# A hybrid decoder layer in split float32: high and low x in one matmul, projections in passes of 256 columns, shorter routing

## The reference

```python
def hybrid_mixer(n, w_in, conv_a_w, ssd_conv_w, ssd_conv_b, ssd_dt_bias, ssd_a_log, ssd_d,
                 ssd_norm_w, w_branch_a, w_branch_b, w_branch_c, w_out):
    u = n @ w_in
    u_a, u_b, u_c, u_g = jnp.split(u, [A_IN, A_IN + B_IN, A_IN + B_IN + SSD_IN], axis=-1)
    y_a = short_conv_mixer(u_a, conv_a_w) @ w_branch_a
    y_b = stick_breaking_attention(u_b) @ w_branch_b
    y_c = mamba2_ssd(u_c, ssd_conv_w, ssd_conv_b, ssd_dt_bias, ssd_a_log, ssd_d, ssd_norm_w) @ w_branch_c
    g_a, g_b, g_c = jnp.split(jax.nn.sigmoid(u_g), 3, axis=-1)
    return (g_a * y_a + g_b * y_b + g_c * y_c) @ w_out
...
    s = jnp.einsum('thcd,hcnd->thcn', q, sub_keys, preferred_element_type=jnp.float32)
    s1, i1 = lax.top_k(s[:, :, 0], PEER_TOPK)
    s2, i2 = lax.top_k(s[:, :, 1], PEER_TOPK)
    cand_s = (s1[..., :, None] + s2[..., None, :]).reshape(ntok, PEER_HEADS, PEER_TOPK * PEER_TOPK)
    cand_i = (i1[..., :, None] * PEER_NKEYS + i2[..., None, :]).reshape(ntok, PEER_HEADS, PEER_TOPK * PEER_TOPK)
    top_s, pos = lax.top_k(cand_s, PEER_TOPK)
```

## Time and profile before

| what | value |
|---|---|
| median of three runs | 3543.44 us |
| the profiled execution's own time | 3542.42 us |
| its span | 3540.7 us |
| PE matmuls busy, weight loads busy | 97%, 89% |
| DVE, ACT, GpSimd busy | 64%, 49%, 1% |
| granted TensorE clock, mean | 0.997 |
| DMA | 178 GB/s |
| A projection | 19.2 to 311.3 us |
| GA, to | 493.8 |
| B with first GB units, to | 815.6 |
| GB, to | 993.4 |
| C, to | 1511.1 |
| GC, w_out and query, to | 1797, 1880, 1987 |
| expert-down, expert-up, to | 2829, 3541 |

### The profile page before, as it was taken

The page is one execution under the profiler, slowest core; times in us unless marked ns, Lnnn a source line. Parts: engine busy times, 40 slices in busy tenths (PEclk is TensorE's granted clock), DMA queues, the critical chain, the costliest instruction groups (busy, mean ns, idle before and its releaser), DMA issues.

```text
span 3540.7 us, 69279 instructions
## 1 busy us (share of the span) xinstructions
PE 3448.7 (97%) x23037; PEld 3166.9 (89%) x23037; DVE 2274.7 (64%) x2901; ACT 1722.0 (49%) x2494; POOL 26.6 (1%) x32
## 2 busy tenths in 40 slices
PE   7999999999999999999999999999999999999998
PEld 7999889998899999978879989899999988887887
DVE  4555444454557777774545999988889855554555
ACT  4444434444445445454445434447777644444444
POOL 0000000000000000000000000000000000000000
PEclk9999999999999999999999999999999999999999
DMA  6666665556666555556677567576666677667665
GB/s 176 176 176 176 189 177 156 157 159 179 192 193 181 175 178 175 172 155 193 189 195 208 149 161 177 157 183 159 159 160 159 164 196 192 193 192 219 195 194 166
DMA packets 484119, 628.62 MB, mean 178 GB/s; under 512 B 76832, under 2 KB 341504, under 8 KB 481792
## 3 DMA queue, kind: packets, MB, share of 16 engines
q1 hardware_dynamic: 483968, 626.59, 64.4%
HBM read 622.03 MB, written 4.26 MB: 177 GB/s over the span
## 4 chain that ended last, share of the span: by engine, by line
PE 79%; DVE 9%; DMA 3%; ACT 3%; issue 3%; SPq 2%; DVEq 0%; ACTq 0%
PE bank L79 25%; PE bank L81 25%; PE bank L80 25%; DVE f_lo L126 2%; PE bank L1715 2%; DVE w_lo L1561 2%; PE bank L2122 2%; DVE w_raw L1554 1%; DMA w_raw<-in_peer_down 1%; SPq L451 1%; DMA f_raw<-in_w_in 1%; DVE c_xc L1182 1%; ACT f_hi L121 1%; DMA f_raw<-in_w_out 0%; SPq L458 0%
## 5 line engine op out<-in xcount | busy, mean ns | idle before, releaser
L126 DVE TENSOR_TENSOR f_lo<-f_raw,f_hi 128x768 fp32r<-128x768 f32 (+2 forms) x640 | 749.2, 1175 | 716.0 <-ACT f_hi L121 715.3
L121 ACT ACTIVATE f_hi<-f_raw 128x768 fp32r<-128x768 f32 (+2 forms) x640 | 646.2, 1016 | 749.3 <-DMA f_raw<-in_w_in 505.4
L79 PE MATMUL bank<-xT_hi,f_hi 128*128 128x256 f32 x2560 | 739.0, 289 | 26.6 <-DVE f_lo L126 11.6
L80 PE MATMUL bank<-xT_lo,f_hi 128*128 128x256 f32 x2560 | 724.3, 283 | 0.0
L81 PE MATMUL bank<-xT_hi,f_lo 128*128 128x256 f32 x2560 | 724.3, 283 | 0.0
L79 PE MATMUL bank<-xT_hi,w_hi 128*128 128x256 f32 x2048 | 590.4, 288 | 19.8 <-DVE w_lo L1561 19.7
L80 PE MATMUL bank<-xT_lo,w_hi 128*128 128x256 f32 x2048 | 579.1, 283 | 0.0
L81 PE MATMUL bank<-xT_hi,w_lo 128*128 128x256 f32 x2048 | 579.0, 283 | 0.0
L1653 DVE TENSOR_TENSOR w_lo<-w_raw,w_hi 128x1024 fp32r<-128x1024 f32 x256 | 313.5, 1225 | 340.8 <-PE bank L81 331.9
L79 PEld LDWEIGHTS bank<-xT_hi,f_hi 128*128 128x128 f32 x2560 | 490.7, 192 | 41.2 <-DVE f_lo L126 16.6
L80 PEld LDWEIGHTS bank<-xT_lo,f_hi 128*128 128x128 f32 x2560 | 491.0, 192 | 1.8 <-issue 1.7
(11 more groups left out here) (268 smaller groups left out, 4856.3 us busy)
## 6 DMA issues: line engine op xcount, KB each, us to landing
w_raw<-in_peer_down SPq DMA_DIRECT2D x1024, 128.0 KB, 3.4
w_raw<-in_peer_up SPq DMA_DIRECT2D x1024, 128.0 KB, 2.6
f_raw<-in_w_in SPq DMA_DIRECT2D x1024, 96.0 KB, 2.4
f_raw<-in_w_in SPq DMA_DIRECT2D x256, 256.0 KB, 2.9
f_raw<-in_w_in SPq DMA_DIRECT2D x384, 128.0 KB, 2.8
f_raw<-in_w_branch_c SPq DMA_DIRECT2D x256, 128.0 KB, 2.8
f_raw<-in_w_branch_a SPq DMA_DIRECT2D x128, 128.0 KB, 2.8
f_raw<-in_w_branch_b SPq DMA_DIRECT2D x128, 128.0 KB, 2.8
```

What stands on the lines that cost most here:

```text
L79: nc.tensor.matmul(out, lhs[0], rhs[0], start=start, stop=False, skip_group_check=True)
L80: nc.tensor.matmul(out, lhs[0], rhs[1], start=False, stop=False, skip_group_check=True)
L121: nc.scalar.activation(self.hi[u % 4][:, 0:cols], self.raw[u % 4][:, 0:cols], ACT.Copy).then_inc(self.hi_done, 1)
L126: nc.vector.tensor_tensor(self.lo[u % 4][:, 0:cols], self.raw[u % 4][:, 0:cols], self.hi[u % 4][:, 0:cols].bitcast(F32), ALU.subtract).the ...
```

## The change

High and low x lie in one tensor `xT`, and `pair_matmul` does high weight by high and low x in one matmul of 512 columns, then low weight by high x over 256 columns into the bank's first half. A block's sum thus fills a whole bank: the first half holds two of the three products, the second the third. The projections run in passes of two blocks: a unit is 4 x 128 rows by 256 columns (1024 columns of a slot, which shrinks from 1280), a pass has four units. A has 3 passes an iteration (12 units), C 5 (20 units), B 2 and a third for v with `tri_matmul` (12). At the end of a pass ACT copies the second half out (`part_a`, `part_qk`, `part_c`) behind the split of the next pass's first unit, and DVE adds the first (`sum_a`, `sum_qk`, `sum_c`).

In C the SSD work is placed anew, all of an iteration's chain within the next: SiLU of x at unit 0, of z at 2, clamp at 3 and 5 (on ACT now, as Relu with a negative scale over one head each), exponents at 4 and 6, PE's turn at 2, states 5, outputs 8, square sum 12; the convolution's first tap goes to ACT (`taps` at 11, 12, 17) and the other three stay on DVE at 14 to 19. In B z moves from 3 to 0, ACT's softplus from 6 to 1, the rest along with it; in GB from unit 4 to 2.

In routing, the rows of keys start a unit earlier and, from unit 32, come every second unit. Of the 256 sums of a head only the 64 that can be in the best 16 are formed, in four rectangles (`RECTS`), two heads at a time. The picks take two instructions a unit from 58 to 97; their ranks are worked back with arithmetic (`side_step`, 98 to 110), and 32 look-ups and 8 reductions (`look_up`, `add_hits`) stand for the 24 keys steps. Three copies after the routing go from DVE to ACT.

```diff
...
-        xT_hi = sb(top, "xT_hi", [P, KD, T], F32R)
-        xT_lo = sb(top, "xT_lo", [P, KD, T], F32R)
+        xT = sb(top, "xT", [P, 2, KD, T], F32R)
+        xT_hi, xT_lo = xT[:, 0, :, :], xT[:, 1, :, :]
+
+        def pair_matmul(out, lhs, k, start, stop):
+            both = out[:, :].rearrange("p (s t) -> p s t", s=2)
+            nc.tensor.matmul(both, lhs[0], xT[:, :, k, :], start=start, stop=False, skip_group_check=True)
+            return nc.tensor.matmul(both[:, 0, :], lhs[1], xT_hi[:, k, :], start=False, stop=stop,
+                                    skip_group_check=True)
...
-                def evacuate_a(p):
-                    act.wait_ge(fl.used, U_AB * p + U_AB)
-                    nc.scalar.activation(c_sb[:, :], bank[1][:, :], ACT.Copy).then_inc(a_evac, 1)
-                    nc.scalar.activation(b_sb[:, :], bank[0][:, :], ACT.Copy).then_inc(a_evac, 1)
+                def part_a(p, r):
+                    act.wait_ge(fl.used, U_AB * p + 4 * r + 4)
+                    for j in range(2):
+                        dst = (c_sb[:, j * T:(j + 1) * T], gate_hid[:, j, 2:T + 2], b_sb[:, j * T:(j + 1) * T])[r]
+                        if r == 1 and first_p(p) and j == 0:
+                            act.wait_ge(a_pad, 1)
+                        nc.scalar.activation(dst, bank[A_PASS[r][1 + j]][:, T:2 * T], ACT.Copy).then_inc(a_part, 1)
...
+                def part_c(p, r):
+                    act.wait_ge(fl.used, C0 + UN * p + 4 * r + 4)
+                    if first_p(p) and r == 0:
                         act.wait_ge(ssd["pad"], 1)
-                    for i in range(3):
-                        nc.scalar.activation(xpad[:, 2 * i:2 * i + 2, 3:T + 3],
-                                             bank[2 + i][:, :].rearrange("p (j t) -> p j t", j=2),
-                                             ACT.Copy).then_inc(ssd["evac"], 1)
-                    for i in range(2):
-                        nc.scalar.activation(zs[:, 2 * i:2 * i + 2, :],
-                                             bank[i][:, :].rearrange("p (j t) -> p j t", j=2),
-                                             ACT.Copy).then_inc(ssd["evac"], 1)
+                    for j in (2 * r, 2 * r + 1):
+                        dst = xpad[:, j, 3:T + 3] if r < 3 else zs[:, j - 6, :]
+                        nc.scalar.activation(dst, bank[C_BANK[j]][:, T:2 * T], ACT.Copy).then_inc(ssd["part"], 1)
...
+                def clamp(p, ch):
+                    act.wait_ge(ssd["ecs"], p + 1)
+                    for h in range(HPG):
+                        here = wts[:, ch, h, :]
+                        nc.scalar.activation(here, here, ACT.Relu, bias=cs_col[:, ch, ds(HPG * p + h, 1)],
+                                             scale=-1.0).then_inc(ssd["clamp"], 1)
+
                 def exp_w(p, ch):
-                    for q in range(2):
-                        act.wait_ge(ssd["min"], 4 * p + 2 * ch + q + 1)
-                        here = wts[:, ch, 4 * q:4 * q + 4, :]
-                        nc.scalar.activation(here, here, ACT.Exp).then_inc(ssd["exp"], 1)
+                    act.wait_ge(ssd["clamp"], 2 * HPG * p + HPG * (ch + 1))
+                    nc.scalar.activation(wts[:, ch, :, :], wts[:, ch, :, :], ACT.Exp, scale=-1.0).then_inc(ssd["exp"], 1)
...
+                def sum_c(p, r):
+                    for j in (2 * r, 2 * r + 1):
+                        here = xpad[:, j, 3:T + 3] if r < 3 else zs[:, j - 6, :]
+                        dve.wait_ge(ssd["part"], 10 * p + j + 1)
+                        nc.vector.tensor_tensor(here, here, bank[C_BANK[j]][:, 0:T], ALU.add).then_inc(ssd["evac"], 1)
...
+                def pass_unit(i, banks):
+                    for kk in range(4):
+                        k = 4 * i + kk
+                        for b in range(2):
+                            at = slice(kk * 256 + b * P, kk * 256 + b * P + P)
+                            last = pair_matmul(banks[b], (fl.hi[i][:, at], fl.lo[i][:, at]), k,
+                                               start=k == 0, stop=k == KD - 1)
+                    last.then_inc(fl.used, 1)
+
                 def a_unit(it, u, begin):
+                    r = u // 4
                     fl.wait_unit(pe, U_AB * it + u)
-                    for m in (2, 3, 0, 1, 4, 5):
-                        if u == 0 and not begin:
-                            if m == 2:
-                                pe.wait_ge(a_evac, 2 * it - 1)
-                            if m == 0:
-                                pe.wait_ge(a_evac, 2 * it)
-                            if m == 4:
-                                pe.wait_ge(a_gh, it)
-                        at = slice(m * P, (m + 1) * P)
-                        last = tri_matmul(bank[m // 2][:, (m % 2) * T:(m % 2 + 1) * T],
-                                          (fl.hi[u % 4][:, at], fl.lo[u % 4][:, at]), (xT_hi[:, u, :], xT_lo[:, u, :]),
-                                          start=u == 0 and m % 2 == 0, stop=u == KD - 1)
-                    last.then_inc(fl.used, 1)
+                    if u % 4 == 0 and not begin:
+                        pe.wait_ge(a_sum, 6 * it - 6 + 2 * r + 2)
+                    pass_unit(u % 4, (bank[A_PASS[r][1]], bank[A_PASS[r][2]]))
...
                 with act.Fori(1, N_AB) as it:
                     for u in range(U_AB):
-                        fl.split_hi(act, B0 + U_AB * it + u, B0 // 4 + 4 * it, u, W_AB)
-                        if u == 0:
-                            copy_qk(it - 1)
-                        if u == 6:
+                        fl.split_hi(act, B0 + U_AB * it + u, B0 // 4 + 3 * it, u, 1024)
+                        if u == 1:
                             softplus(it - 1)
-                        if u == 12:
+                        if u in (4, 8):
+                            part_qk(it, u // 4 - 1)
+                        if u == 7:
                             weights_b(it - 1)
-                        if u == 15:
+                        if u == 10:
                             o_hi_b(it - 1)
                 branch_split("gb", GB0, KD, GB_PAIRS, gb_hook)
...
+                def pick_row(g):
+                    if 13 <= g < QU:
+                        return g - 13
+                    return 19 + (g - QU) // 2 if QU <= g < QU + 26 and (g - QU) % 2 == 0 else None
+
...
+                def sums(q):
+                    r = head(2 * q)
+                    for i0, i1, nj, at in RECTS:
+                        ni = i1 - i0
+                        v.tensor_tensor(cand[:, r:r + 2, at:at + ni * nj].rearrange("p h (a b) -> p h a b", b=nj),
+                                        sides[:, r:r + 2, 0, i0:i1].unsqueeze(3).to_broadcast([P, 2, ni, nj]),
+                                        sides[:, r:r + 2, 1, 0:nj].unsqueeze(2).to_broadcast([P, 2, ni, nj]),
+                                        ALU.add).then_inc(t_cand, 1)
+
+                def best_step(o):
...
+                def look_up(side, a):
+                    dve.wait_ge(t_side, (7, 13)[side])
+                    dve.wait_ge(t_diff, 2)
+                    k = 0 if a < 4 else 4 if a < 8 else 8
+                    ranks = side_f[:, side, :].rearrange("p (r k) -> p r k", k=PK)
+                    v.scalar_tensor_tensor(out=hit[side][:, a, :, k:PK], in0=ranks[:, :, k:PK], scalar=float(a),
+                                           in1=keys_of[:, :, side, a:a + 1].to_broadcast([P, R, PK - k]),
+                                           op0=ALU.is_equal, op1=ALU.mult).then_inc(t_hits[side], 1)
+
...
+                def add_hits(side, c):
+                    dve.wait_ge(t_hits[side], PK)
+                    k0, k1, a, r0, r1 = ((0, 4, 4, 0, R), (4, 8, 8, 0, R), (8, 16, 16, 0, PH), (8, 16, 16, PH, R))[c]
+                    v.tensor_reduce(key_of[:, side, :].rearrange("p (r k) -> p r k", k=PK)[:, r0:r1, k0:k1],
+                                    hit[side][:, 0:a, r0:r1, k0:k1].rearrange("p a r k -> p r k a"),
+                                    AX.X, ALU.add).then_inc(t_red, 1)
 
                 def q_lo(n):
...
```

747 lines of the change are left out of this document (388 added, 359 removed).

## The result

The changed kernel takes **3608.5 us**, the median of four runs (3606.2 to 3612.0), against 3541.8 for the kernel before in the same comparison: a ratio of **1.019** (95% interval 1.0174 to 1.0206), some 67 us slower. The forecast was 3554 and its range ended at 3581: the direction was right, the size was wrong, and the time lies outside the range. The profiled execution took 3611.95 us.

A forecast was written before the change was run, and what follows sets the result against it. It took TensorE (PE), 79% of the chain, to bound the kernel, and DVE the routing. Terms of -14.6, +4, +1.4, +41.8, +3.5, -25 and 0.5 in the query phase gave +11.6 on 3542.4: 3554 us, range 3514 to 3581.

The forecast's parts named there:

- Term 4, C: C stage: a period grows from 65.9 to 71.6 us through PE's waits for splits; +41.8 us, the merged matmul's saving included.
- walk: Unit-by-unit sum of ACT and DVE durations in C: waits of 9.9 us and restarts of 0.3 a period.
- Units 13 to 19: End of a C iteration: unit 13 waits 0.8 us, then DVE's 22.1 us against PE's 19.4 cost 2.7.
- Term 1, the merged matmul: Projections in A, B and C: 2560 products each cost 0.3467 us instead of 0.36; -34.1 us.
- a fixed part per run of columns: Rival 2, projections: the merged matmul pays a fixed part for each run and saves nothing, 3588 us; 5%.
- Term 2, A: A stage: 277.5 us against 292.1, with 0.44 lost at each of 23 pass ends; -14.6 us.
- Term 3, B: B stage: softplus makes unit 2's split 2.0 us late, an iteration takes 41.1; +4 us, and +1.4 in the next branch.
- Term 5: GC, behind C: its first units carry the last scan, and two table loads of 1.28 enter inv_rms; +3.5 us.
- Term 6, routing: Routing: DVE bounds it, and with less DVE work the loss falls from 32 to 7 us; -25 us.
- the ring covers the walk: Rival 1: up to four units of lead hide the waits, wholly 3483 us (7%) or half of C's gaps 3517 (17%); 24%.
- SiLU starts late: Rival 3, C: SiLU waits for the last conv piece, which lengthens unit 1's wait; period 75, 3581 us; 13%.
- three signs: Wrong if C's period stays under 68, the merged matmul's successor starts after more than 0.23, or routing stays over 300 us.

The follow-up runs named there:

- Both fillers: Unneeded matmuls put into PE's waits in C: at units 1 and 4 of the changed kernel, 3599.7 us; at unit 1 of best1_silu0, 3541.3 us.
- softplus_later: The changed kernel with ACT's softplus in B behind the split of unit 3 instead of 1, DVE's behind 4 instead of 3: 3595.5 us.
- route_only: The kernel before with the new routing alone, projections and scan unchanged: 3524.9 us, ratio 0.9943.
- best2: The changed kernel with copies, sums, softplus, SiLU, clamp, norm and scan loads moved to other units, and the square sum a unit earlier: 3493.6 us, 0.9856.
- best1_silu0: The changed kernel with ACT's and DVE's work reordered (3503.8 us), but last copies and SiLU of x put back at unit 0 in C: 3552.6 us.

## Why the prediction was wrong

**Term 4, C, is the step that failed.** Its walk adds waits and 0.3 us of "restarts" to a period, and so takes a wait at its length. The waits came as walked: 2.88 for 3.0 at unit 1, 2.10 for 2.3 at unit 4, 74 us in C for 71. What was left out stands behind them. PE's granted clock fell to 0.50 behind 11 of the 14 waits of 2.1 us and more in C, and 58 pairs pay 0.3 us each, 17 us; the first matmuls behind the 68 gaps, a good tenth of a us each and 0.36 behind the longest where the clock had fallen, and the merged pair's pitch are 13.5 more than before, where the term had 2. Together with 3 us of gaps this is the miss of 31. Both fillers show the clock's part with the wait kept: 13 us of C in one, 11 of the whole in the other. The C stage of the kernel before couldn't show it, for its longest wait of PE is 0.8 us and its clock 1.00. But its trace has it elsewhere: behind the 2.7 us wait in GC a window gives 0.50, third from the end, and it is not among the rows that the prediction read.

```profile
1552.90:1556.20 3.30, 3.30 (x9) 2.65 (x8) 3.30 (x7) 1.58 (x4) 0.00 (x0) 0.50 0.02 7
```

**Units 13 to 19** were walked as 0.8 for the first and 2.7 for the rest (its list adds up to 22.1 only with the sums of both passes that end there). Measured are 1.0 and, in units 14, 15, 16 and 18, 2.8 on the mean. The size is right; the reason, DVE's load alone, is right in part. Unit 15's wait varies from 0.3 to 1.8 us: there ACT waits for a weight's DMA, behind 1 MB that SP loads for the scan between two units. In the period shown this held DVE up by hardly 0.1 us, in the next one by 1.2; from there to unit 16's wait of 1.1 DVE works without a break:

```profile
1263.76 1.06 ACT L130 ACTIVATE f_hi<-f_raw 128x1024 fp32r<-128x1024 f32 x1 [3.33 <-DMA f_raw<-in_w_in]
```

**Term 1, the merged matmul,** was booked at 34 us and is worth 12 to 18 in two pairs of kernels (15 and 16 by the medians). The 0.2267 of the earlier trace rows doesn't hold for the merged matmul: its mean is 0.2335, and the matmul behind gives 0.0036 back. By the starts 18 to 25 us are left, and the rest, so I take it, goes where PE waits for the split anyway; this was not separated. The rival "a fixed part per run of columns", saving nothing, is excluded by both intervals, and so are the 34. By the Trainium skill, "TensorE: Matmul & The Clock Gate", section "Back-to-back issue gap", the gap of an isolated matmul is N / 2.4 + 2.5 ns, and by it 6.4 us would have been saved (an estimate from that page). The starts save 0.007 to 0.010 a product, not 0.0025, so the measurement decides against that rule here too, though the second interval of the whole time (4 to 20) reaches down to 6.4.

**Term 2, A,** gave -10.2 at its end for -14.6: per product 0.003 more than the pitch used (0.350 for 0.3467), 768 x 0.003 = 2.5 of the 4.4 missing; the rest is not accounted for. The pass's ends came as walked, 0.29 to 0.35 of wait and 0.1 of slow start.

**Term 3, B:** an iteration takes 41.58 where the walk had 41.1, and 43.09 where the clock fell. softplus_later shows that the wait is the one named. The miss of 6 us in this stage is four times 0.5 and twice 2.0.

**Term 5** met its number, +3.6 for +3.5, but that was luck in part: PE's waits in GC grew by 2 us (7.4 to 9.4), and the longest, 3.0 us, is C's wait for SiLU of x carried over, which the term didn't name.

**Term 6, routing,** read DVE as the bound and asked what is left when DVE has less to do; it said 7 us of loss. route_only gives -19 for -25 (-14.6 in its profile from the start of the query projection on), and in the changed kernel it is -12.6. DVE's waits for expert rows grew from 9.4 to 24.2 us, and without half of the traffic 14 us of query and routing go. A rival was missing: the transfer late next. The row that bears on it, DVE waiting 9.4 us for rows, is in the trace of before and not among those of the prediction. The reductions also cost more than their bound: 2.0 us for the "up to 1.17" (below).

**The rivals.** That the ring covers the walk is excluded by C's 74 us of gaps. "SiLU starts late", period 75, has the size right (74.2 to 78.2) by the wrong mechanism: the wait is 2.88, no longer than forecast. Of the three signs by which I said I would be wrong, one came, a merged matmul followed after more than 0.23; routing, at 313 - 12.6, stands at the edge of the other.

**Where the expected gain went.** The parts that save, merging (15) and routing (19), are real, and best2, which keeps both, ends 49 under before; the other 15 of the 49 were not split up. It also shows what the placement of ACT's and DVE's work cost in the change, 115 us.

## What to carry to other kernels

A wait of PE is charged with its length and with what follows it: look at the granted clock in the few us behind the longest waits of before, and where a change adds waits like those of 2.1 to 4.2 us here, allow for matmuls behind them at half pace (behind 11 of 14 in C, and behind all those of 4.2 in best1_silu0). Where an engine works in a written order, a copy or activation that needs the end of a group of matmuls belongs at least one split behind the place where its operand is ready; such pieces one or two units later were worth 13 to 49 us here. When the bound engine is relieved, take the next wait from the trace of before, however small it is, as the new bound, transfers too.

## What was not expected of the hardware

- The granted clock was 0.50 for 5.4 us behind an idle time of PE of 2.88 us, and 0.55 for 3.6 us behind one of 2.10. Not behind each: in C it fell behind five of seven waits of 2.8 to 2.9 and six of seven of 2.1; in B, behind the same wait of 1.8, in some iterations and not in others (43.09 and 41.58 us). Behind a wait of 1.27 with unneeded matmuls ahead of it, it didn't fall.
- A 512 column matmul whose moving operand lies in two runs is followed after 0.230 to 0.241 us, one over 512 columns in a row after 0.2267. No run changes the two runs alone, so that they are the cause isn't shown.
- A reduction on DVE over 1024 elements read with a stride takes 2.0 us (the row below, after the change), the one of the kernel before over 1024 in a row 1.17:

```profile
L1626 DVE TENSOR_REDUCE key_of<-t_hit 128x64 f32<-128x1024 f32 x4 | 8.0, 2000 | 0.0
```
